# First modulation vectors formed on TensorE from whole-row weight loads

## What is computed

```python
c_act = jax.nn.silu(c)
for l in range(DEPTH):                       # DEPTH = 1
    mod = c_act @ w_ada[l] + b_ada[l]        # w_ada: 1024 x 6144
    sh1, sc1, g1, sh2, sc2, g2 = [m[:, None, :] for m in jnp.split(mod, 6, axis=-1)]
    h = _rmsnorm(x, norm_attn_g[l]) * (1.0 + sc1) + sh1
    proj = h @ w_in[l]                       # w_in: 1024 x 3600
...
```

## Time and profile before

| | us |
|---|---|
| median of three runs | 3629.4 |
| lowest and highest of them | 3621.26, 3639.6 |
| the profiled execution | 3635.35 |
| its span in the trace, first to last instruction | 3633.3 |
| PE busy in the span | 3441.9 (95%) |
| DVE busy | 2148.4 (59%) |
| ACT busy | 1031.6 (28%) |

### The profile page before, as it was taken

How to read it: one execution, slowest core, us unless ns; L and a number is a source line. 1 busy time by engine, 2 the same in 40 slices (tenths; PEclk the granted TensorE clock), 3 DMA queues, 4 the chain that set the end, 5 groups by cost and what they waited for, 6 DMA issues and landing times. The chain is left out here.

```text
span 3633.3 us, 49233 instructions
## 1 busy us (share of the span) xinstructions
PE 3441.9 (95%) x19911; PEld 2821.2 (78%) x19911; DVE 2148.4 (59%) x4936; ACT 1031.6 (28%) x1604; POOL 131.9 (4%) x116
## 2 busy tenths in 40 slices
PE   5988899999999999899999999989999999999998
PEld 4655867887888888774688888878888886578887
DVE  6554656567667575764455667676766636543334
ACT  3354023222321212243432121222122124432222
POOL 0012010000000000100000000010000010000000
PEclk9998979999999999898999999989999999999999
DMA  8532024444234343330023434333343413023331
GB/s 176 148 96 64 4 74 125 118 132 115 85 91 116 99 115 94 99 85 18 24 62 99 113 93 111 101 106 87 107 107 102 109 49 111 12 76 95 97 99 64
DMA packets 646938, 333.94 MB, mean 92 GB/s; under 512 B 31659, under 2 KB 642935, under 8 KB 646456
## 3 DMA queue, kind: packets, MB, share of 16 engines
q1 hardware_dynamic: 645812, 330.63, 33.4%
q10 hardware_dynamic: 900, 0.18, 0.0%
HBM read 328.61 MB, written 2.77 MB: 91 GB/s over the span
## 5 line engine op out<-in xcount | busy, mean ns | idle before, releaser
L2099 PE MATMUL psum<-hn_high,high 128*128 128x512 f32 (+1 forms) x3136 | 1116.1, 356 | 9.7 <-DVE low L2544 9.7
L2101 PE MATMUL psum<-hn_high,low 128*128 128x512 f32 (+1 forms) x3136 | 1110.5, 354 | 0.0
L2100 PE MATMUL psum<-hn_low,high 128*128 128x512 f32 (+1 forms) x3136 | 1107.5, 353 | 0.0
L2629 DVE SCALAR_TENSOR_TENSOR partial<-stage,cond,partial 128x128 f32<-128x128 f32 x2592 | 701.9, 346 | 0.0
L2099 PEld LDWEIGHTS psum<-hn_high,high 128*128 128x128 f32 x3136 | 591.6, 189 | 120.5 <-issue 21.0
L2100 PEld LDWEIGHTS psum<-hn_low,high 128*128 128x128 f32 x3136 | 591.7, 189 | 86.5 <-issue 0.5
L2101 PEld LDWEIGHTS psum<-hn_high,low 128*128 128x128 f32 x3136 | 591.1, 188 | 82.8
L2544 DVE TENSOR_TENSOR low<-stage,high 128x1024 fp32r<-128x1024 f32 (+2 forms) x415 | 493.1, 1208 | 187.8 <-ACT high L1771 187.3
L1771 ACT ACTIVATE high<-stage 128x1024 fp32r<-128x1024 f32 (+2 forms) x415 | 415.2, 1025 | 504.0 <-DMA stage<-in_w_ffn 354.8
L2099 PE MATMUL psum<-hidden_high,high 128*128 128x512 f32 (+1 forms) x1408 | 495.8, 352 | 2.0 <-DVE hidden_low L2549 2.0
L2101 PE MATMUL psum<-hidden_high,low 128*128 128x512 f32 (+1 forms) x1408 | 496.4, 353 | 0.0
(11 more groups left out here) (316 smaller groups left out, 2948.3 us busy)
## 6 DMA issues: line engine op xcount, KB each, us to landing
stage<-in_w_ffn SPq DMA_DIRECT2D x240, 512.0 KB, 4.2
stage<-in_w_ada SPq DMA_DIRECT2D x768, 128.0 KB, 2.8
stage<-in_w_in SPq DMA_DIRECT2D x48, 512.0 KB, 4.5
stage<-in_w_out SPq DMA_DIRECT2D x24, 512.0 KB, 4.1
stage<-in_w_ffn SPq DMA_DIRECT2D x32, 384.0 KB, 3.8
stage<-in_w_gate SPq DMA_DIRECT2D x22, 512.0 KB, 3.9
stage<-in_w_up SPq DMA_DIRECT2D x22, 512.0 KB, 5.1
stage<-in_w_down SPq DMA_DIRECT2D x16, 512.0 KB, 4.0
```

Source lines behind the costliest of these rows:

```text
L2099: self.e.matmul(out, high[:, i], xh, start=first and n == 0, stop=False)
L2100: self.e.matmul(out, high[:, i], xl, start=False, stop=False)
L2101: done = self.e.matmul(out, low[:, i], xh, start=False, stop=last and n == nk - 1)
L2629: self.e.scalar_tensor_tensor(acc, view[:, k, :], by, acc, ALU.mult, ALU.add).then_inc(*inc)
```

## The change

1. In the opening, the 16 modulation blocks become 16 blocks of one row per partition and 1024 columns (`load`: row 8 p + k to partition p). Each is one DMA with runs of 4096 bytes. The bytes are the same, 512 KB each.
2. PE forms the vectors: eight float32 matmuls per block, each with 128 columns of the block as the stationary operand and one column of SiLU(c) as the moving one (`open_products`). All accumulate into 16 columns of one PSUM bank, and one DVE addition of the bias (`open_vectors`) ends them. The 16 DVE passes over blocks, the four pairs of `quarter` matmuls and the four bias additions go.
3. SiLU of the first condition vector comes from an own small load with 8 values per partition (`cond_first`, `open_condition`). The other condition steps move to j = 13.
4. The tokens are issued before the rows of small vectors; the distance tables are loaded in `setup`; the first vector tile is turned at j = 3, the others at j = 13; the distance matmuls come one step earlier.

All later modulation vectors are made as before.

```diff
@@ Walk.load
-        if isinstance(k0, tuple):
+        if isinstance(k0, tuple) and cols > P:
+            moves = [(dst, w.rearrange("(p r) n -> p r n", r=KT)[:, k0[0]:k0[0] + nk, c0:c0 + cols])]
+        elif isinstance(k0, tuple):
@@ Walk.setup
         self.load_first()
-        self.take_condition(0)
-        self.take_vectors(0, 1)
+        self.open_condition()
         self.load_start()
+        self.distance_tables()
@@ Walk.first_block
-        squares = []
+        squares, opening = [], self.mix.next()
         for j in range(2 * KT):
-            one(j)
+            k, half = j % KT, 1 - j // KT
+            n, stage, view = self.weights(i["w_ada"][0], (k,), 1, half * D, D, split=False)
+            self.open_products(j, n, view[:, 0, :], half, k, opening)
+            stage.free = [("opened", j)]
             if j == 3:
+                self.take_vectors(0, 1)
+            if j == 13:
+                for c in range(3):
+                    self.take_condition(c)
                 self.take_vectors(1, 3)
-                self.take_condition(1)
-                self.take_condition(2)
...
-            if k == KT + 1:
+            if k == KT:
                 self.distance_bias()
...
-        self.finish_modulation()
+        self.open_vectors(opening, mod[:, 0:2 * KT, 0], bias[:, 0:2 * KT])
+        opening.free = self.mod_ready = [("opened_vectors",)]
@@ Sync.load_first
         self.dma(self.misc(), ("eye",), self.mem.eye[:], self.mem.const["eye"])
+        self.dma(self.misc(), ("tokens", "main"), self.mem.tokens_main, self.mem.inp["x"][0].rearrange("(a p) n -> p a n", p=P))
@@ Scalar.load_conditions
+        self.e.dma_start(self.mem.cond_first[:, 0, :], i["c"][0].rearrange("(p r) -> p r", r=KT)) \
+            .then_inc(self.sems["cond_landed"], 16)
@@ Tensor
+    def open_products(self, j, n, w, half, k, bank):
+        self.wait_ge("landed", n)
+        self.wait_ge("cond_first_silu")
+        if j == 0:
+            self.wait_free(bank)
+        for b in range(KT):
+            at = half * KT + b
+            done = self.e.matmul(bank.ap[:, at:at + 1], w[:, b * P:(b + 1) * P], self.mem.cond_first[:, 1, k:k + 1],
+                                 start=j == b == 0, stop=k == KT - 1, skip_group_check=True)
+        done.then_inc(*self.mark("opened", j))
@@ Vector
+    def open_vectors(self, bank, mod, bias):
+        self.wait_ge("opened", 2 * KT - 1)
+        self.wait_ge("vec", 0)
+        self.e.tensor_tensor(mod, bank.ap[:, 0:2 * KT], bias, ALU.add).then_inc(*self.mark("opened_vectors"))
```

More of the change, by code:

```diff
@@ L248, in start_maps @@
         self.cond_rows = self.area("cond_rows", 3 * QROWS).rearrange("p (c n) -> p c n", c=3)
+        self.cond_first = self.area("cond_first", 2 * KT).rearrange("p (c n) -> p c n", c=2)
         self.table = self.area("table", SKEW)[0:N_BUCKETS + 1]
@@ L788, in distance_bias @@
     def distance_bias(self):
-        self.distance_tables()
         for o, n in ((0, 512), (512, SKEW - 512)):
@@ L1607 @@
     modulation_vector = clear = load_start = turn_vectors = condition = turn_tokens = distance_tables = idle
-    load_first = load_conditions = distance_rows = store_distances = skew_distances = token_square = token_pair = token_pair_sums = turn_context = gate_logs = gate_sums = gate_exps = turn_gates = load_bias = attention_scores = attention_turn = attention_values = idle
+    open_condition = open_products = open_vectors = load_first = load_conditions = distance_rows = store_distances = skew_distances = token_square = token_pair = token_pair_sums = turn_context = gate_logs = gate_sums = gate_exps = turn_gates = load_bias = attention_scores = attention_turn = attention_values = idle
     attention_normalise = head_square = head_roots = head_spread = gains = clear_pads = gate_row = idle
@@ L1631, in load_start @@
         col = lambda ap: ap.rearrange("(n o) -> n o", o=1)
-        self.dma(self.misc(), ("tokens", "main"), mem.tokens_main, i["x"][0].rearrange("(a p) n -> p a n", p=P))
         self.dma(self.misc(), ("small", 0), mem.dt_bias, col(i["dt_bias"][0]))
@@ L1811, in load_conditions @@
         i = self.mem.inp
+        self.dma_counts["cond_landed"] = 16
+        self.e.dma_start(self.mem.cond_first[:, 0, :], i["c"][0].rearrange("(p r) -> p r", r=KT)) \
+            .then_inc(self.sems["cond_landed"], 16)
+        self.board.new["cond_first",] = "cond_landed", 16
         for n, c in enumerate((i["c"][0], i["c_2"][0], i["c_ctx_2"])):
-            sem, rows = "cond_landed" if n == 0 else "conds_landed", c.rearrange("(p r) -> p r", r=QROWS)
+            sem, rows = "conds_landed", c.rearrange("(p r) -> p r", r=QROWS)
             for q in range(4):
@@ L1817, in load_conditions, with open_condition @@
             self.board.new["cond_rows", n] = sem, self.dma_counts[sem]
+    def open_condition(self):
+        self.wait_ge("cond_first")
+        self.e.activation(self.mem.cond_first[:, 1, :], self.mem.cond_first[:, 0, :], ACT.Sigmoid) \
+            .then_inc(*self.mark("cond_first_sigmoid"))
     def condition(self, n, x, t):
-        self.wait_ge("cond_rows", 2 if n else 0)
+        self.wait_ge("cond_rows", 2)
         self.wait_free(t)
@@ L2608, in scale_tile, with open_condition @@
             .then_inc(*self.mark("scaled", name, k))
+    def open_condition(self):
+        raw, act = self.mem.cond_first[:, 0, :], self.mem.cond_first[:, 1, :]
+        self.wait_ge("cond_first_sigmoid")
+        self.e.tensor_tensor(act, raw, act, ALU.mult).then_inc(*self.mark("cond_first_silu"))
+    def open_vectors(self, bank, mod, bias):
+        self.wait_ge("opened", 2 * KT - 1)
+        self.wait_ge("vec", 0)
+        self.e.tensor_tensor(mod, bank.ap[:, 0:2 * KT], bias, ALU.add).then_inc(*self.mark("opened_vectors"))
     def modulation_sums(self, name, n, view, part, vectors, quarter):
```

## The result

Over 6 runs of each kernel, the one before has a median of 3634.5 us (3621.26 to 3647.12) and the changed one 3659.93 us (3646.9 to 3665.76). The ratio is 1.006, with a 95% interval of 1.0033 to 1.0086: **21.8 us slower** by the ratio, between 12 and 31; the two medians lie 25.4 us apart. Its profiled execution took 3653.03 us with a span of 3651.0, so 17.7 us over the span of before.

A forecast was written before the change was run, and what follows sets the result against it. DVE's multiply-add chain was taken to bound the opening until 59.38 us; PE's new chain, 8.9 + 73.1 + 0.35 + 0.04 = 82.4 us, adds 23.0 us to the 3629.4 us median: 3652.4 us, range 3640 to 3667.

The forecast's parts named there:

- What bounds the opening: Opening, 59.54 us: DVE's 120 multiply-adds bound it until 59.38 before the change, PE's queue after it.
- The start of the chain: Opening: PE starts near 8.9 us, once DVE's product for SiLU of the first condition ends near 8.85.
- The chain: Opening, PE's one queue of matmuls, transposes, sums and small steps: 73.1 us at 0.215 us an instruction.
- the new matmuls: Opening, PE: 16 x 8 x 2 = 256 instructions at 0.215 us, 55.0 us.
- Four sums over partitions: Opening, PE: 32 instructions at 0.215 us, 6.9 us.
- Stalls inside it at nothing, loads at nothing: Opening: no waits inside PE's queue, and faster 4 KB runs give nothing, since PE asks only 154 GB/s.
- The limit that the prediction named: Opening, block loads: the cover against stalls would be gone if a block's load took longer than 3.4 us.
- The sum: Whole kernel: end of the opening moves by +23.0 us, 3652.4 us against the median of 3629.4.
- The clock: Opening, PE: stays at 1.2 GHz from 8.9 to 82 us, judged by durations rather than the clock column.
- rival A: Opening, PE: clock rises soon, instructions every 0.11 us or so, 10.8 us less than before, 3618.6 us; chance 0.05.
- Rival B: Behind the opening: half of 7.8 us of `w_in` waits, 4 us, given back, 3648.5 us; chance 0.08.
- Rival C: Opening, new loads at half of 223 GB/s: 4.7 us a block, vectors near 97, 3667 us; chance 0.04.

The follow-up runs named there:

- experiment 1: Kernel before with only the changed order of tokens, rows, tables and turns, DVE still multiplying: 3637.7 us beside 3633.34, first product at 58.31.
- experiment 2: Changed kernel with only the first 128 columns of every second block multiplied, 72 of 128 matmuls, all loads kept: 3643.36 us, first product at 64.31.
- experiment 5: Changed kernel with each block loaded by two DMAs so that runs are 512 bytes again: 3652.8 us, first product at 85.46.
- experiment 7: Whole-row DVE multiply-adds in the changed order, but each block loaded by two DMAs in 512-byte runs: 3625.04 us, first product at 55.28.
- experiment 3: Changed kernel with six unused bf16 matmuls of 512 columns before each block's products: 3657.95 us, first product at 84.10.
- experiment 4: Changed kernel with operands exchanged, SiLU column stationary and 512 block columns moving, two matmuls a block: 3632.55 us, first product at 61.37.
- experiment 6: Changed kernel's order and whole-row loads, but DVE multiplies and adds each 128 x 1024 block, PE sums each half: 3618.74 us beside 3633.34.
- experiment 8: Whole-row DVE kernel with POOL adding token squares, vectors turned at j = 5 and 9, distances at j = 10: 3619.4 us, ratio 0.9945 against before.

## Why the prediction was right

**What bounds the opening.** Right for the changed kernel: the vectors come when PE's queue ends, and DVE and the DMAs are out of the way. Of the kernel before the prediction said that until 59.38 it is DVE's chain. That left out the 5.37 us in which DVE waited for the root, behind distance tables that had been loaded late (experiment 1). It did no harm to the sum, which priced the new chain whole.

**The start of the chain.** Predicted 8.9, measured 9.19. DVE's product started at 8.88, where the prediction had it end near 8.85, and PE started 0.14 us behind its end.

**The chain.** Predicted 73.1 us and a tail of 0.35, measured 71.99 with the tail. The term that was mis-sized, slightly, is the new matmuls' 55.0 us: from the start of each group to that of the next they take 53.5, and 53.8 with the tail of the last. The price of 0.215 us came from groups of eight with waits close by the earlier trace rows; in long groups it is 0.213, and the group that follows starts a little closer. Four sums over partitions took 6.3 us where 6.9 were put, since the next group starts 1.57 us after the start of each; the distance matmuls took 2.23 from start to start, not 1.9. Experiment 2 shows that the count times the spacing gives the cost to within 0.4 us.

**Stalls inside it at nothing, loads at nothing.** Right in the changed kernel. The limit that the prediction named wasn't one, though: a block lands 3.6 us after its issue (the median), longer than the 3.4 us of a step, and PE never waited, since a block is asked for three steps before it is needed. The cover was thinner than I had it: when experiment 2 gave PE less to do, it waited 1.9 us for the fifth block, which lands behind the tokens. The 512-byte runs cost nothing on PE (experiment 5) and some 4 us on DVE (experiment 7). For the same blocks in the same order, with the DMA engines full, the queue moved 294 GB/s with short runs and 357 with long ones from 24 to 30 us (228 and 405 from 17 to 20); the 223 and 412 of the earlier trace rows compared other transfers and have a larger ratio than either. The Trainium skill's page "DMA: Bandwidth & Descriptors" (Specifications) has 512 bytes suffice for the full rate: by it experiment 7 would show no loss. It shows one of 4.4 us, of which 0.5 is the clock's, and twice as many DMAs may have a part in it. So the measurement speaks against the page here and doesn't settle it. The expectation, from the rows of before, was 5.6.

**The sum.** Predicted +23.0 us at the first product, measured +21.85. Predicted 3652.4 us against a median of 3629.4; the six runs of each kernel have medians of 3659.93 and 3634.5, 7.5 and 5.1 us higher, and the ratio gives 21.8 us (12 to 31). That 21.8 and 21.85 agree so closely is partly luck: the difference of the medians is 25.4, and the one profiled pair of executions gives 17.7. Against that pair alone the step from opening to span would look wrong; the 4.1 us lie in the wander behind the opening.

**The clock.** Right, and this decided the sign: at the fast pace rival A had the time 10.8 us below that of before. The durations, not the column, told that the opening runs at 1.2 GHz, and 72 us of PE work without a gap did not change it. Experiments 3 and 4 show the other side: with operands of 512 moving columns at the start the clock rose between 11.9 and 13.8 us and at 14.3 us, PE having started at 9.36 and 9.29. Rival A, and the rule "activity releases the throttle" of the Trainium skill's page "TensorE: Matmul & The Clock Gate" (What's actually happening), fall for one-column float32 matmuls in this program: PE was busy without a gap from 9.19 to 81.18 at 1.2 GHz, and rose only behind the first matrix products (0.63 us for one until 88.5, 0.39 from 89.3). For 512 moving columns the traces of experiments 3 and 4 agree with it.

**Rival B** (given back behind the opening). Its sign did show in the profiled pair: a first product 21.85 us later and an end only 17.7 later, less than the 19 that the prediction named. Its mechanism didn't: ACT's waits for `w_in` in the first 52 us behind the opening went up, from 7.8 us before (60 to 112) to 9.6 (82 to 134), and at 340 us the shift is 24.0, more than at the first product. What is lost of it later is as large as the wander between other runs. The interval of 12 to 31 us can't rule B's 19 out. **Rival C** (slow loads) fell: the 512 KB blocks land in 3.6 us, and no wait of PE in the opening ends with a DMA.

**What I missed.** The change is a gain and a loss in one. Its order alone ends the opening 5.75 us earlier (experiment 1), nearly all of it by the distances; only the sum over the new chain made that unnecessary to know for the time, but a reader of the prediction could think that nothing in the change helps. Two expectations had the same fault: in experiments 1 and 6 I moved DVE's start and counted its work, and left out that its queue has copies and sums between the passes which wait for late rows and for a slow PE.

## What to carry to other kernels

A float32 matmul with 128 x 128 weights and one moving column shows up here as two instructions, each with a weight load beside it (335 of each in the opening with the transposes, 70.05 us busy for the loads and 71.99 for the matmuls), and work of this shape did not raise the clock even in 72 us without a gap. So try a matrix-vector product on PE with the matrix as the moving operand (first product at 61.37 instead of 85.91), or on an engine that sweeps it in long passes (50.88). Before moving work to an idle engine, multiply its instruction count by the spacing in the trace at the clock that the durations show, and compare with the whole stretch, not with the work it replaces. When an in-order engine starts earlier, look for the copies between its passes and for what they wait for. And when a reordering gains time, look where: here it was a small table on the way to the root of the mean, not the engine that started earlier.

## What was not expected of the hardware

- The granted clock reads 1.00 in the opening at both paces: for one-column instructions at 0.213 us and for 512 columns at 0.43 us. Until the column changes for the first time, only durations tell them apart.
- In experiment 3 the clock fell at 53 us under a mixture that had held it up for 40 us, rose for a block at 63.5 and fell again. In experiment 6 it was up for the sum at 23.21 us behind nothing but transposes. Why isn't settled in either.
- DVE over 128 x 1024 beside a working POOL took 1.97 us instead of 1.28, and POOL's addition of 128 x 512 up to 2.1 instead of 1.27, with both operands of each in SBUF. Their ends alternate at some 1.1 us: the two work one after the other, not side by side.
- The same program ends between 3621 and 3654 us. From the first matrix product to the end, with no change there, the traces of the eleven kernels take 3565.1 to 3577.3 us, and the mean granted clock doesn't order them: 3567.6 us at 0.956 (experiment 7), 3575.9 at 0.963 (experiment 8).
